# Three phases of a fused block on one core: who issues the bias copies, how densely the weight splits are packed, and where key/query products and output products sit in the attention heads

## What is computed

```python
h = rms_norm(x, norm_gain)
proj = h @ w_in                       # pool_v, pool_g, q, k, v, attn_g, 512 wide each
y_pool = multiscale_pool(pool_v, pool_w, pool_scale) * silu(pool_g)
y_attn = chunked_rel_attention(q, k, v, rel_bias) * silu(attn_g)   # 8 heads of 64
x = x + concat([y_pool, y_attn]) @ w_out
return rms_norm(x, final_norm_gain)
```

## Time and profile before

| | us |
|---|---|
| median of three runs | 1687.26 (1686.40 to 1687.45) |
| the profiled execution, its own time | 1687.45 |
| its span in the trace | 1685.7 |
| PE busy in the span | 1618.0 (96%) |
| DVE, ACT, POOL busy | 1064.6, 835.5, 691.8 |

### The profile page before, as it was taken

One profiled execution on the slowest core, in us unless ns is written; L12 is line 12 of the kernel. 1 busy time (PEld: TensorE's weight loads), 2 busy tenths in 40 slices (PEclk: granted clock), 3 DMA queues, 4 the chain that ended last, 5 costly groups with the idle time before them and its releaser, 6 DMA issues. The chain is left out here.

```text
span 1685.7 us, 44263 instructions
## 1 busy us (share of the span) xinstructions
PE 1618.0 (96%) x17920; PEld 1219.7 (72%) x17920; DVE 1064.6 (63%) x2188; ACT 835.5 (50%) x1580; POOL 691.8 (41%) x734
## 2 busy tenths in 40 slices
PE   4999999999999999999988999999999999999986
PEld 2545545558677776777767888889888899888864
DVE  7777677647565566557346666666666666666664
ACT  5655555422121111112125677767777767777674
POOL 2545445311101111112413555555555555555553
PEclk8999999999999999999998999999999999999998
DMA  5564664564524532452854524444334444344331
GB/s 212 204 232 166 202 234 162 216 245 150 212 68 172 198 147 79 176 189 98 232 186 131 154 85 134 139 141 140 119 103 133 146 139 144 87 134 132 104 123 51
DMA packets 131201, 257.87 MB, mean 153 GB/s; under 512 B 15512, under 2 KB 61096, under 8 KB 128952
## 3 DMA queue, kind: packets, MB, share of 16 engines
q1 hardware_dynamic: 129960, 253.74, 44.7%
q0 software_dynamic: 1040, 1.31, 0.4%
HBM read 151.33 MB, written 83.48 MB: 139 GB/s over the span
## 5 line engine op out<-in xcount | busy, mean ns | idle before, releaser
L2092 POOL TENSOR_TENSOR stages<-stages 128x512 f16<-128x512 f32 (+2 forms) x368 | 364.0, 991 | 366.4 <-ACT stages L1929 366.2
L1561 PE MATMUL bank<-middle,weights 128*128 128x128 f16 x1792 | 313.2, 220 | 2.1 <-DVE entry L1208 0.9
L1564 PE MATMUL bank<-middle,weights 128*128 128x128 f16 x1792 | 313.1, 220 | 0.0
L1563 PE MATMUL bank<-middle,weights 128*128 128x128 f16 x1792 | 313.0, 220 | 0.0
L1923 ACT ACTIVATE stages<-bank,log_ps 128x512 f32<-128x512 f32 (+2 forms) x368 | 221.6, 602 | 161.9 <-PE bank L1816 97.0
L1763 DVE CUSTOM_DVE_ANT_0 stages<-bank,stages 128x640 bf16<-128x640 f32 (+4 forms) x256 | 198.7, 776 | 76.0 <-PE bank L1728 75.8
L977 PE MATMUL bank<-middle 128*128 128x256 f16 x784 | 213.7, 273 | 3.7 <-DVE stages L1117 3.7
L979 PE MATMUL bank<-middle 128*128 128x256 f16 x784 | 213.7, 273 | 0.0
L980 PE MATMUL bank<-middle 128*128 128x256 f16 x784 | 213.7, 273 | 0.0
L1929 ACT ACTIVATE stages<-stages 128x512 f16<-128x512 f32 (+2 forms) x368 | 202.8, 551 | 11.7
L1793 PE MATMUL bank<-entry,stages 128*128 128x512 f16 x768 | 193.3, 383 | 2.5 <-DVE stages L1984 2.5
(11 more groups left out here) (147 smaller groups left out, 3613.0 us busy)
## 6 DMA issues: line engine op xcount, KB each, us to landing
entry<-in_x SPq DMA_DIRECT2D x64, 512.0 KB, 3.7
h_ops<-middle SPq DMA_DIRECT2D x16, 1792.0 KB, 6.1
middle<-h_ops SPq DMA_DIRECT2D x112, 256.0 KB, 6.0
middle<-h_ops SPq DMA_DIRECT2D x49, 512.0 KB, 7.1
middle<-middle SPq DMA_DIRECT2D x384, 64.0 KB, 2.0
residual<-entry SPq DMA_DIRECT2D x32, 512.0 KB, 2.8
entry<-residual SPq DMA_DIRECT2D x30, 512.0 KB, 5.4
out<-entry SPq DMA_DIRECT2D x30, 512.0 KB, 2.6
```

The source lines that it names most:

```text
L1561: nc.tensor.matmul(dst, wh, hop3[:, o, 0, kt, :], start=(kt == 0 and s < 2 and pair == 0), stop=False, skip_group_check=True)
L1563: nc.tensor.matmul(dst, wh, hop3[:, o, 1, kt, :], start=False, stop=False, skip_group_check=True)
L1564: mm = nc.tensor.matmul(dst, wl, hop3[:, o, 0, kt, :], start=False, stop=(kt == 3), skip_group_check=True)
L2092: nc.gpsimd.tensor_tensor(p_l[:, h % 2, c + a:c + b], p32[g][:, a:b], p_h[:, h % 2, c + a:c + b], ALU.subtract).then_inc(A["pl_done"], 1)
```

## The change

1. The two bias copies go from SP's list at the start of the q phase to ACT's list in the h phase, behind `v12_hi(5)`.
2. `wk_at` spreads a part over two steps (pieces 0 to 3, then 4 to 6) in place of three; parts begin at steps 8, 10, ..., 22. `take_c12` stands before the third piece of the step.
3. `move_q(sp, 0, half)` comes one residual block later.
4. In the attention, tile t computes the keys and the queries of tile t + 1 in slots 0 to 13 (tile 0 only its queries, in slots 0 to 6), and the output of the tile before in slots 15 to 22, six matmuls at a time. Slots 14 and 23 stay empty, and in tile 0 slots 7 to 23. They are split in heads 2 and 4. The squares and the end of the tile before go to heads 6 and 7 and to head 0 of the next tile.
5. SP's list of the attention is put in another order. In tile 0 it waits for all four quarters of the output weights, and then loads `hop3` and moves.

```diff
+                if p == BIAS_AT + 2:
+                    act.wait_ge(H["ext_stored"], 16)
+                    for r, (dst, width) in enumerate(((bq_dram, 640), (bk_dram, 256))):
+                        act.dma_start(dst, bass.AP(rel_dram.tensor, ...)).then_inc(H["bias_stored"], 16)
...
-            i = (m - WK_FIRST) // 3
+            i = (m - WK_FIRST) // 2
-            return i, (range(0, 3), range(3, 5), range(5, 7))[(m - WK_FIRST) % 3]
+            return i, (range(0, 4) if (m - WK_FIRST) % 2 == 0 else range(4, 7))
...
-                    if j == parts[-1]:
+                    if j == parts[2]:
                         take_c12(m)
...
-            sp.wait_ge(H["ext_stored"], 16)
-            for r, (dst, width) in enumerate(((bq_dram, 640), (bk_dram, 256))):
-                sp.dma_start(dst, bass.AP(...)).then_inc(H["bias_stored"], 16)
...
-                if b == 0:
+                if b == 1:
                     for half in range(2):
                         move_q(sp, 0, half)
...
         def kq_slot(t, h, a):
-            x = SLOTS * h + a
-            if t < LAST and x < PRODUCTS:
-                return 2 * t + 3, x
-            first = 9 if t == 0 else 17
-            return (2 * t + 4, x - first) if t + 2 < ATILES and first <= x < first + PRODUCTS else None
+            x = SLOTS * h + a + (PRODUCTS if t == 0 else 0)
+            return divmod(x, PRODUCTS) if t < LAST and x < 2 * PRODUCTS else None
         def split_at(t, h):
-            if t == LAST or h not in ((0, 2) if t > 0 else (2,)):
-                return None
-            return 2 * t + 2 + h // 2
+            if t == 0:
+                return 3 if h == 2 else None
+            return {2: 2 * t + 2, 4: 2 * t + 3}.get(h) if t < LAST else None
...
+            return (t - 1, (x - 15) // 2, (x - 15) % 2) if t > 0 and 15 <= x < 23 else None
...
         def squares_at(t, h):
+            return {6: ((t - 1, 0),), 7: ((t - 1, 1),)}.get(h, ()) if t > 0 else ()
         def finish_at(t, h):
+            found = ((t - 2, 1),) if t > 1 and h == 0 else ()
+            return ((t - 1, 0),) if t > 0 and h == 7 else found
...
         def a_phase_sp(sp):
                 if t == 0:
                     for n in range(NKT):
                         load_wob(n)
-                        for s in ((), (0, 1), (2, 3, 4), (5, 6))[n]:
-                            load_hop3(sp, 2, s)
+                    sp.wait_ge(A["wob_lo"], NKT)
                 else:
+                    move_k(sp, t, 1)
+                    move_q(sp, t, 1)
                     load_v(sp, t)
                     load_gate(sp, t, 1)
...
+                if t < LAST:
+                    for s in range(4 if t + 2 < ATILES else 0):
+                        load_hop3(sp, t + 2, s)
+                    move_k(sp, t + 1, 0)
+                    for s in range(4, PRODUCTS if t + 2 < ATILES else 0):
+                        load_hop3(sp, t + 2, s)
+                    load_gate(sp, t + 1, 0)
+                    move_q(sp, t + 1, 0)
```

More of the change, by code:

```diff
@@ L1490, in output_slot @@
                 if 7 <= x < 15:
[L1491 to L1497, removed]
+                    return t - 1, (x - 7) // 2, (x - 7) % 2
+                return (t, x - 18, 0) if 18 <= x < 22 else None
+            return (t - 1, (x - 15) // 2, (x - 15) % 2) if t > 0 and 15 <= x < 23 else None
         def round_at(t, h):
@@ L1507, in squares_at @@
         def squares_at(t, h):
[L1509 to L1510 removed]
+            if t == LAST:
+                return {3: ((t - 1, 0),), 5: ((t - 1, 1),)}.get(h, ())
+            return {6: ((t - 1, 0),), 7: ((t - 1, 1),)}.get(h, ()) if t > 0 else ()
         def finish_at(t, h):
[L1514 to L1515 removed]
+            found = ((t - 2, 1),) if t > 1 and h == 0 else ()
+            if t == LAST:
+                return {4: ((t - 1, 0),), 6: ((t - 1, 1),)}.get(h, found)
+            return ((t - 1, 0),) if t > 0 and h == 7 else found
         def res_of(t):
@@ L1773, in a_phase_pe, with output @@
         def a_phase_pe(pe):
-            def output(t, i, first, end):
+            def output(t, i, half):
                 j, n2 = i // 2, i % 2
-                if first == 0:
+                if half == 0:
                     pe.wait_ge(A["ytl_done"], 2 * t + (1 if t == LAST else 2))
@@ L1785, in output @@
                     if i < 2 and t < LAST:
-                        pe.wait_ge(A["kq_u"], 5 * min(2 * t + 6, 2 * ATILES) - 1 + i)
+                        pe.wait_ge(A["kq_u"], 5 * min(2 * t + 6, 2 * ATILES))
                 elif t == LAST:
                     pe.wait_ge(A["ytl_done"], 2 * t + 2)
-                for m in range(first, end):
+                for m in range(6 * half, 6 * half + 6):
                     kt, p = m // 3, m % 3
@@ L1793, in output @@
                     mm = nc.tensor.matmul(out_bank(t, i), yh, w, start=(m == 0), stop=(m == 11))
-                if end == 12:
+                if half == 1:
                     mm.then_inc(A["out_mm"], 1)
@@ L1859, in other @@
                     for pair in range(2):
-                        kq_half(pe, w // 2, 2 * (PRODUCTS * (w % 2) + s) + pair)
-                for part in output_slot(t, h, a):
-                    output(*part)
+                        kq_half(pe, t + 1, 2 * (PRODUCTS * w + s) + pair)
+                if output_slot(t, h, a):
+                    output(*output_slot(t, h, a))
             def head(t, h):
@@ L1893, in a_phase_pe @@
             for i in range(4):
-                output(LAST, i, 6, 12)
+                output(LAST, i, 1)
         def a_phase_act(act):
@@ L2051, in other @@
                     if s in KQ_TAKES:
-                        kq_take(dve, w, KQ_TAKES[s])
-                for of, i, _, end in output_slot(t, h, a):
-                    if end == 12:
+                        kq_take(dve, 2 * t + 2 + w, KQ_TAKES[s])
+                if output_slot(t, h, a):
+                    of, i, half = output_slot(t, h, a)
+                    if half == 1:
                         residual(of, i)
@@ L2147, in a_phase_sp @@
                         sp.dma_start(res_last[:, j, :], r_dram[2 * LAST + j]).then_inc(last_loaded[j], 16)
-                    continue
-                if 0 < t < ATILES - 2:
-                    for s in range(PRODUCTS):
-                        load_hop3(sp, t + 2, s)
-                move_k(sp, t + 1, 0)
-                move_q(sp, t + 1, 0)
-                load_gate(sp, t + 1, 0)
                 if t > 0:
                     for j in range(2):
-                        store(t - 1, j)
-                move_k(sp, t + 1, 1)
-                move_q(sp, t + 1, 1)
+                        load_residual(t - 1, j)
+                if t < LAST:
[6 more added lines that the diff above has]
+                    move_q(sp, t + 1, 0)
             for t in (LAST - 1, LAST):
```

14 lines of the change are left out of this document (6 added, 8 removed).

## The result

The changed kernel takes 1746.66 us (median of 4 runs, 1744.5 to 1749.3), the kernel before beside it 1686.83: a ratio of 1.0353, 95% interval 1.0338 to 1.0369. The prediction said slower (0.94) and 1727, with 1705 to 1742 as its range; the time lies above that range. The profiled execution of the changed kernel took 1741.65 us with a span of 1739.9, 5 us less than the median of its four runs.

What follows compares the result with a forecast made beforehand. The prediction took PE's list as the bound, PE being busy 96% of the span. Its terms, 4 + 8.5 + 3.5 + 8 + 5.8 + 9.7 + 0.5 = 40 us, added to 1687.45 gave 1727 us, range 1705 to 1742.

Steps and rivals of the forecast that it cites:

- Step 1: h phase: bias copies on ACT block it 9 us, and PE waits at transposes; +4 us.
- Step 2: q phase: weight parts beginning at k = 0 arrive late, three PE waits for one; +8.5 us (5 to 11).
- Step 3: First maxima: PE waits longer for `move_q`, now behind a store and a load; +3.5 us (2 to 5).
- PE idle 6 us: Sign to look for in the trace: PE idle 6 us ahead of the first maxima.
- Step 4: Tile 0: SP's chain makes the moves late, PE waits some 9 us despite seven fewer products; +8 us (5 to 10).
- Step 5: Tiles 1, 14 and start of 15: relocated products and output matmuls lengthen tiles 1 and 14; +5.8 us (4 to 7).
- Step 6: Tiles 1 to 14: the next tile's queries come 0 to 1.1 us late in each; +9.7 us (0 to 16).
- 7: Values in the attention: `load_v` follows 12 moves but still lands about 1.3 us ahead of need; +0.5 us (0 to 3).
- ACT is held as long as SP was: Rival, h phase: ACT's lateness goes on into pair 7, 12 us in place of 4, with slow moves; 1741 us, chance 0.11.
- The faster rival: Attention: the emptied tile 0 pays, with idle time in tiles 0, 14 and 15 gained; −6.2, 1681 us, chance 0.03.

Runs made afterwards that it cites:

- the better kernel: The kernel before with two edits of SP's list alone, the early load of the step 20 weight part and early moves of tile 0's queries: 1676.19 us, ratio 0.9939.

## Why the prediction was right and wrong

**Step 1, mis-sized: 10.9 by the traces in place of 4.** The prediction had the possibility (the second copy holds ACT, which holds back `copy_p1`, `normalise` and the transposes) and its own upper bound, 7 to 9 us. It took 9 us of blocking, where the row of the same copy on SP said 11.51, and explained that row by seven transfers queued ahead. The experiments say otherwise: on SP behind the same seven loads, without the query copy between, its issue took 0.78 us. The copy is held by the one that stands right ahead of it. The price of the traffic was underrated more: the sentence that 3.6 MB more move at that time had no number in the sum, and the query copy alone, with no hold, costs 9 us. By the Trainium skill (DMA: Bandwidth & Descriptors, "Issuing engines are not separate DMA queues") the transfers of all issuing engines interleave on the same 16, and the runs agree: a copy issued by ACT pushed a load issued by SP from 9.1 to 17.5 us. The prediction quoted that rule and left it out of the sum. The same section calls the issuing time "usually small"; here the second copy's was 11.53 us, and the measurement decides.

**Step 2, right in place and total, the total partly by luck.** 8.5 predicted, 7.2 in the traces, 9 by undoing it. Its mechanism, the place in SP's list, was shown by moving the load. But its three waits, 5.8, 3.9 and 3.9 with their refilling, were 2.36, 1.84 and 3.05, and the sum had no term for the time at 1.2 GHz behind two of them, some 3.4 us of the 7.2.

**Step 3, the number right, by luck.** The seam is 3.9 us longer for 3.5 predicted, but that is a cost of 8 to 9 less 4.7 that the attention part gives back there, of which the prediction had neither. PE waits 6.31 us for the moves, as it said ("PE idle 6 us"). The step was not undone alone in the changed kernel; the opposite edit is part of the better kernel.

**Step 4, right in kind.** PE's wait for the moves is 9.65 us (predicted "about 9"), and the granted clock was 0.76 in the mean of that tile, part of it at 1.2 GHz; the tile grew by 5.9 instead of 8. With SP's old order it is back at 42.5 us, so the cost is that of SP's list.

**Step 5, right.** Tile 14 is as long as a full one, and with tile 1 and the end the step adds up to 5.0 with the waits for `attend` taken out.

**Step 6, the mechanism right and its size too large here, for it was hidden.** Its arithmetic put PE at the maxima of head 0 at 11.19 us behind the mark and the moves at 11.15 to 12.25. In the trace PE arrives 0.75 us later, since it has waited once for `attend` in between, and only tiles 1 and 2 show a wait (0.27 and 1.01 us). With the empty third slots filled, late queries appear, 0.3 to 1.3 us in five tiles, and a longer window removes them. Their mean was estimated too high as well: in that run three of tiles 3 to 13 are longer than 51.6 us, by 0.5 to 1.0, and all eleven together by 2.3, where the sum had 0.6 for each tile; tiles 1 to 14 together are 5.1 longer than with the longer window, where the sum had 9.7.

**The step that is missing.** The working priced an empty slot as time saved (1.30 us for a half output, moved elsewhere) and never asked what the slot had covered. The heads without fillers in the third slot were taken at b = 2.69 us from heads that had all their slots full. The wait stands in the code of `scores`, ahead of the matmuls. None of the full tiles before leaves a third slot empty, so no row of a full tile shows it. But the list of waits of the kernel before had it, three times, and one of them in tile 14, whose last heads have empty third slots: the prediction read that tile's length and not what PE waited for in it. I named "a wait in the full tiles that I have not seen" as what would make the prediction wrong, and that is what it was: 20 of the 54 us in the traces.

**The sum.** 40 us predicted, 54 in the traces, 60 in the medians. Add 20.2 for `attend` and 6.9 for step 1, take off 8.5 for step 6 and 4.3 for the others (1.3, 2.1, 0.8 and 0.5 less in steps 2, 4, 5 and 7, 0.4 more in step 3), and one is at 54.3. The 5 us between the profiled execution and the median lie in the spread of this kernel: 26 executions of it took 1741.65 to 1751.25 us, and the profiled one was the fastest.

**Rivals.** That ACT is held as long as SP was came true on the row, and 1741 was the nearest of the rivals, but by a sum without `attend`. The faster rival, that the emptied tile 0 pays, is refuted: even with SP's old order there the tile is as long as before.

## What to carry to other kernels

Before a filler is moved out of a slot, look at what its neighbours need in that slot: a slot of 1.3 us of work may be what hides 0.7 us of another engine, and an empty slot next to it costs nothing. Where two waits lie behind each other, the first hides the second; a term that is "late by 0 to 1 us" appears only when the one ahead of it is gone. Look in the list of waits for a wait that so far occurs only where a slot is empty. Hold a mended change against the kernel before with the same mends. Give a large copy a price in bytes for the loads that are issued behind it, not only one for its issue: here the engine held for 11.5 us was the visible part, and letting it go won nothing.

## What the runs showed of the hardware

- Of two DRAM to DRAM copies of 1024 rows each, one right behind the other in the same queue, the second's issue took 10.2 to 11.7 us on SP (seven kernels) and 10.3 to 11.5 on ACT (eight). Without the other ahead of it the same copy took 1.22 us on ACT and 0.78 on SP behind seven loads, and 20 us behind it 0.65. The size of its rows isn't the reason, since it is the smaller of the two.
- The query copy alone (2560 KB) made one of eight loads of 512 KB land after 17.5 us, where its like took 9.1 beside the key copy (1024 KB). Both are single traces.
- In the q phase waits of 2.36 and 3.05 us were followed by 3.4 us at 1.2 GHz in the changed kernel; one of 1.84 us there, and one of 3.13 us at the same place in the kernel before, were not.
- Groups of six small SBUF to SBUF transfers with nothing ahead of them on the queue took 3.66 to 5.05 us to issue. The slow ones among the first halves of the queries are mostly the same in three kernels (tiles 4, 6, 9 and 14).
